# Hosted experts of the second joint stage in pairs of groups: eight products, one GELU, two groups' weights, eight accumulations

## The chip, the cores and the metric

The kernel runs on one core of a Trainium2 chip. A core has five engines that run side by side, each with its own in-order list of instructions: TensorE (PE, matrix products into PSUM), VectorE (DVE, elementwise work and reductions), ScalarE (ACT, activation functions and copies), GpSimd (POOL, here the issuer of gathers) and SyncE (SP, here the issuer of all other transfers). They wait for one another by semaphores only. Transfers run on 16 DMA engines that all issuers share. The metric is device time in microseconds, median over runs of the whole program; all data is float32.

## The reference

One layer of a hybrid encoder for 1024 prompt tokens and 8 x 16 sample tokens, nine tiles of 128 tokens in all. Each token passes a gated mLSTM branch (4 heads of 256) and a forgetting attention branch "FoX" (16 heads of 64), then an expert layer (PEER) and a gate. What matters here is the expert layer: each token picks 8 x 16 = 128 of 16384 single-neuron experts, each with a row `u` and a row `v` of 1024 numbers.

```python
idx = (take_along_axis(i1, j // PEER_TOPK) * PEER_KEYS + take_along_axis(i2, j % PEER_TOPK))
g = jax.nn.softmax(sc, axis=-1)
act = jax.nn.gelu(jnp.einsum('thkd,td->thk', u_tab[idx], xb).astype(jnp.float32), approximate=False)
return jnp.einsum('thk,thkd->td', (g * act).astype(xb.dtype), v_tab[idx])
```

and of the attention, for a block of 128 queries: `s = q k / 8 + c_q - c_k`, masked, `softmax(s)`, times `v`.

## The kernel before

The program is a sequence of stages. Six of the nine tiles have their experts gathered row by row by the class `Experts`: three in a first instance, `ex0`, "hosted" inside two joint stages, whose main work is something else, and three in the last joint stage (`stage_experts`), beside a dense form of the experts of the other three tiles. The first joint stage projects the input (`stage_project`) and hosts groups 0 to 51 of `ex0`. The second is the later part of attention (`stage_attend` with `b0` = 2, `b1` = 8: six query blocks, 96 steps) and hosts the remaining groups 52 to 95, 44 of them. It runs from about 1830 to 2525 us.

A group is four experts (`G` = 4) for 128 tokens, one token on each partition. For each expert POOL issues one indirect gather (`fetch`, L2558) that puts the rows `u` and `v`, 8 KB for each token and 1.05 MB together, into one of eight slots of `ex_uv`: two groups of four slots, group g in slots g % 2 * 4 and after. The fetch of group g + 2 into a slot waits until the accumulation of group g with that slot is counted in `added`. Then, on DVE, a group is nine units (`dve_unit`):

- units 0 to 3: one product each (L2599), the dot of `u` with the token's vector, into `ex_dot`; each waits for its slot's fetch (`uv_in`) and adds to `dotted`;
- unit 4: the weights (L2606), the four GELU values times the gates, after `geluted`;
- units 5 to 8: one accumulation each (L2615) of weight times `v` into `ex_acc`; each adds to `added`.

The GELU of a group is one ACT instruction on four numbers a partition (L2642), placed in ACT's list where unit 3 stands. Gelu and Exp are in different function tables, and an ACT_TABLE_LOAD stands before each change of table: one before a GELU, one before the next Exp, which is the softmax numerator (`act_exp`, L617).

Where hosted units stand among the attention's work is fixed as the program is written out. Each of the 96 steps has two halves; `hosted(s, half)` asks `units` for the half's share of the 44 x 9 = 396 units, 2 or 3 of them, in order of group and unit. In a step, DVE takes the maximum of the scores (L586) that PE left in PSUM, then the reciprocal of a sum, then a slot of the mLSTM, then the first half's units, another mLSTM slot and the second half's units. ACT's list has the Exp, the copies of the transposed probabilities (L625), the mLSTM's parts and, by the same `hosted`, the GELUs. Its list, too, is in order: what stands behind a GELU waits with it. SP loads the operands of later heads and chunks from `scratch_z` in pieces of 384 to 512 KB and stores results; POOL only issues fetches in this stage.

Of the kernel before, what the change touches and what calls it, by code (L numbers as in the profile page):

```python
# [18 lines left out]
ACT = mybir.ActivationFunctionType  # L19
# [608 lines left out]
class MlstmPrompt:  # L628
# [48 lines left out]
    def rows(self, c):  # L677
        t = self.c0 + 1 + c
        return slice(t * P, (t + 1) * P)

    def sp_load(self, sp, c):
        z, rows = self.z, self.rows(c)
        if c >= 1:
            self.wait_full(sp, self.group(c - 1, "q1"))
        sp.dma_start(self.q[:], z[rows, C_QM:C_KM]).then_inc(self.q_in, 16)
        if c >= 1:
            sp.wait_ge(self.kw_set, c * H_M)
        sp.dma_start(self.k[:], z[rows, C_KM:C_VM]).then_inc(self.k_in, 16)
        if c >= 1:
            sp.wait_ge(self.y_head, c * H_M)  # L690
        sp.dma_start(self.o[:], z[rows, C_OM:C_IM]).then_inc(self.o_in, 16)
        if c >= 1:
            self.wait_full(sp, self.group(c - 1, "c1", H_M - 1))
        sp.dma_start(self.v[:, :, 0:DM], z[rows, C_VM:C_OM].rearrange("t (h e) -> t h e", h=H_M)).then_inc(self.v_in, 16)
# [368 lines left out]
def stage_attend(nc, K, z, bias, cache_lf, gates, ck_last, C, m, T, b0, b1, ex=None, g0=0, g1=0):  # L1063

    with Stage(nc, f"att{b0}") as st:
        fx = FoxPrompt(nc, K, st, z, T, b0, b1)
        ml = MlstmPrompt(nc, K, st, z, gates, C, m, T, b0, b1)
        t0 = b0 + 1 if b0 else 0
        ga = Gates(K, st, z, bias, cache_lf, gates, ck_last, T, t0, b1 + 1 - t0, fx)
        STEPS = fx.STEPS  # L1070
        PER_STEP = ml.SLOTS * (b1 - b0) // STEPS
        assert PER_STEP == 2
        slot = lambda s, half: divmod(2 * s + half, ml.SLOTS)

        def hosted(s, half):
            return ex.units(g0, g1, 2 * s + half, 2 * STEPS) if ex and s < STEPS else []

        block = st.ctx.enter_context(nc.Block())

        @block.sync  # L1080
        def _(sp):
            ga.sp_load(sp)
            fx.sp_first(sp)
            ml.sp_load(sp, 0)
            if ex:
                ex.load_ahead(sp, g0)
            ga.sp_sums(sp)
            fx.sp_sums(sp)
            ga.sp_rest(sp)
            for s in range(STEPS):  # L1090
                fx.sp_step(sp, s)
                for half in range(2):
                    ml.sp_step(sp, *slot(s, half))
                    for g, unit in hosted(s, half):
                        ex.rows_unit(sp, g, unit)
            fx.sp_last(sp)
            ml.sp_last(sp)
            ga.sp_last(sp)
            if ex:
                ex.rows_end(sp, g1)  # L1100

        @block.tensor
        def _(pe):
            for g in range(len(fx.groups)):
                fx.pe_head(pe, 0, g)
            ga.pe_turn(pe)
            ga.pe_scores(pe)
            for s in range(STEPS + 1):
                if s < STEPS:
                    fx.pe_scores(pe, s)  # L1110
                    for hd, g in fx.heads_at(s):
                        fx.pe_head(pe, hd, g)
                    ml.pe_slot(pe, *slot(s, 0))
                if s >= 1:
                    for r in range(fx.rounds(s - 1)):
                        fx.pe_turn(pe, s - 1, r)
                if s < STEPS:
                    ml.pe_slot(pe, *slot(s, 1))
                if s >= 1:
                    for r in range(fx.rounds(s - 1)):  # L1120
                        fx.pe_mix(pe, s - 1, r)

        @block.scalar
        def _(act):
            for g in range(len(fx.groups)):
                fx.act_head(act, 0, g)
            ga.act_first(act)
            ga.act_probs(act)
            for s in range(STEPS + 2):
                if s >= 2:  # L1130
                    fx.act_y(act, s - 2)
                if s < STEPS:
                    for hd, g in fx.heads_at(s):
                        fx.act_head(act, hd, g)
                    ml.act_slot(act, *slot(s, 0))
                if 1 <= s <= STEPS:
                    for r in range(fx.rounds(s - 1)):
                        fx.act_probs(act, s - 1, r)
                if s < STEPS:
                    fx.act_exp(act, s)  # L1140
                for g, unit in hosted(s, 0):
                    ex.act_unit(act, g, unit)
                if s < STEPS:
                    ml.act_slot(act, *slot(s, 1))
                for g, unit in hosted(s, 1):
                    ex.act_unit(act, g, unit)

        @block.vector
        def _(dve):
            ga.dve_first(dve)  # L1150
            fx.dve_first(dve)
            ml.dve_first(dve)
            for s in range(STEPS + 1):
                if s < STEPS:
                    fx.dve_max(dve, s)
                if s >= 1:
                    fx.dve_invert(dve, s - 1)
                if s < STEPS:
                    ml.dve_slot(dve, *slot(s, 0))
                for g, unit in hosted(s, 0):  # L1160
                    ex.dve_unit(dve, g, unit)
                if s < STEPS:
                    ml.dve_slot(dve, *slot(s, 1))
                for g, unit in hosted(s, 1):
                    ex.dve_unit(dve, g, unit)
            if ex:
                ex.dve_close(dve, g1)
            ga.dve_last(dve)

        if ex:  # L1170
            @block.gpsimd
            def _(pool):
                ex.pool_span(pool, g0, g1)


class FoxSample:
# [3 lines left out]
    STEPS = 2 * NSEQ  # L1180
# [770 lines left out]
class Spread:  # L1951
# [25 lines left out]
    def units(self, i, a, b):  # L1977
        n = (i - self.FROM) * self.PER_STEP
        return range(n + a, n + b) if 0 <= n < self.UNITS else range(0)
# [544 lines left out]
class Experts:  # L2524

    G = 4
# [107 lines left out]
    def act_unit(self, act, g, unit):  # L2634
# [3 lines left out]
        if unit == self.G - 1:  # L2638
# [2 lines left out]
                act.wait_ge(self.weighed, g - 1)  # L2641
            act.activation(self.act[:, g % 2, :], self.dot[:, g % 2, :], ACT.Gelu).then_inc(self.geluted, 1)  # L2642

    def rows(self, t):
        return slice((self.tile0 + t) * P, (self.tile0 + t + 1) * P)

# [32 lines left out]
    def units(self, g0, g1, at, of):  # L2679
        n = (g1 - g0) * self.UNITS  # L2680
        for u in range(n * at // of, n * (at + 1) // of):
            yield g0 + u // self.UNITS, u % self.UNITS


class Dense:
# [500 lines left out]
```

## Time and profile before

| what | value |
|---|---|
| median of 3 runs | 4817.47 us (4817.3 to 4831.1) |
| profiled execution | 4826.2 us, span 4824.5 us |
| DVE busy, whole span | 2995.7 us (62%) |
| PE busy, whole span | 4326.6 us (90%) |
| ACT busy, whole span | 999.4 us (21%) |
| second joint stage | about 1830 to 2525 us |

The page of the profile gives busy times over the whole span and a chain of work that ended last; that chain reaches back only through the last stage. So a stage in the middle is read from its own stretch: busy time of each engine in it, the lists of waits ("A <- B" says that group A stood idle until group B released it), and the timeline of single instructions. An engine's idle time costs something only if the engine is the one that the stage waits for. Granted clock is the share of TensorE's full 2.4 GHz, 0.5 being its lower level of 1.2 GHz.

### The profile page before, as it was taken

Reading aid. Unit: us, or ns where it says so; the run is one execution under the profiler, and the core shown is the slowest. Engines: PE = TensorE matmul, PEld = TensorE weight load, DVE = VectorE, ACT = ScalarE, POOL = GpSimd, SP = SyncE. Lnnn points to the kernel's source line nnn. Section 1 sums busy time; section 2 is a strip of 40 time slices with the busy share of each in tenths; the row PEclk is TensorE's granted clock in tenths of the full one; section 3 lists DMA queues with packets and bytes.
Section 4 is the critical chain, followed back from the end, with each engine's and each line's share of the span. In section 5 each row is a group of like instructions: output and inputs, shape, how many; then the busy total and the mean of one; then the engine's idle time right before and its main releaser. Section 6 shows DMA issues by size and latency. Waiting matters only on the chain. (4 is left out here: it accounts for less than half of the span.)

```text
span 4824.5 us, 49007 instructions
## 1 busy us (share of the span) xinstructions
PE 4326.6 (90%) x16974; PEld 2667.5 (55%) x16974; DVE 2995.7 (62%) x6257; ACT 999.4 (21%) x1991; POOL 1260.4 (26%) x969
## 2 busy tenths in 40 slices
PE   8997686989999996888887988869999999999988
PEld 5555453665555554666664666654545454544534
DVE  1002241458777767888870587767888777777733
ACT  1113321111001104555551122220000000000023
POOL 0000031014444442333320000004444444444400
PEclk9998788999999997878878999989999999999999
DMA  4443496769999998988958777749999999999941
GB/s 169 143 147 98 146 320 265 284 236 421 385 382 391 384 355 284 335 307 313 343 209 331 278 267 262 241 155 418 419 407 408 419 419 419 416 414 409 418 177 58
DMA packets 363496, 1477.74 MB, mean 306 GB/s; under 512 B 38338, under 2 KB 178418, under 8 KB 242706
## 3 DMA queue, kind: packets, MB, share of 16 engines
q0 software_dynamic: 119872, 824.76, 42.4%
q1 hardware_dynamic: 193874, 625.13, 34.9%
q10 hardware_dynamic: 49536, 25.17, 1.7%
q8 instruction: 112, 1.84, 0.2%
q14 instruction: 102, 0.84, 0.0%
HBM read 1369.00 MB, written 115.38 MB: 308 GB/s over the span
## 5 line engine op out<-in xcount | busy, mean ns | idle before, releaser
L2558 POOL DMA_INDIRECT ex_uv<-in_uv,idx x768 | 1169.6, 1523 | 1683.4 <-DVE ex_acc L2615 1487.8
L2599 DVE CUSTOM_DVE_ANT_0 ex_uv<-ex_uv,ex_xp 128x1024 f32<-128x1024 f32 x768 | 912.9, 1221 | 296.2 <-DMA ex_uv<-in_uv,idx 249.6
L2615 DVE SCALAR_TENSOR_TENSOR ex_acc<-ex_uv,ex_wt,ex_acc 128x1024 f32<-128x1024 f32 x768 | 943.0, 1281 | 10.3 <-DVE C L897 3.2
L392 PE MATMUL proj_psum_acc<-proj_w,aT_later 128*128 128x385 f32 x2304 | 748.7, 487 | 8.0 <-DMA proj_w<-in_w_in 8.0
L2813 PE MATMUL exp_psum_dn<-exp_dn_big,exp_dn_gg 128*128 128x512 f32 x1536 | 686.6, 597 | 28.3 <-DVE exp_dn_gg L2769 28.1
L2804 PE MATMUL exp_psum_dn<-exp_dn_xT,exp_dn_big 128*128 128x384 f32 x2048 | 684.3, 488 | 7.6 <-DMA exp_dn_big<-in_ud 7.6
L392 PEld LDWEIGHTS proj_psum_acc<-proj_w,aT_later 128*128 128x128 f32 x2304 | 437.0, 190 | 319.3 <-DMA proj_w<-in_w_in 8.2
L2804 PEld LDWEIGHTS exp_psum_dn<-exp_dn_xT,exp_dn_big 128*128 128x128 f32 x2048 | 390.5, 191 | 307.7 <-issue 71.2
L2813 PEld LDWEIGHTS exp_psum_dn<-exp_dn_big,exp_dn_gg 128*128 128x128 f32 x1536 | 291.8, 191 | 379.1 <-issue 351.5
L301 PE MATMUL proj_psum_acc<-proj_w,aT 128*128 128x385 f32 x1152 | 377.1, 488 | 4.2 <-DMA proj_w<-in_w_in 2.3
L301 PEld LDWEIGHTS proj_psum_acc<-proj_w,aT 128*128 128x128 f32 x1152 | 218.3, 190 | 158.9 <-issue 4.5
L2242 PE MATMUL rt_psum_b<-rt_w,rt_yT 128*128 128x512 f32 x576 | 265.7, 623 | 31.8 <-ACT rt_yT L2335 24.3
L2277 PE MATMUL rt_psum_b<-rt_xT,rt_w 128*128 128x128 f32 x2304 | 265.8, 279 | 4.1 <-ACT rt_xT L2335 4.1
L2277 PEld LDWEIGHTS rt_psum_b<-rt_xT,rt_w 128*128 128x128 f32 x2304 | 264.7, 196 | 5.4 <-issue 5.4
L552 PE MATMUL att_psum_fs<-att_fkT,att_fqT 65*128 65x512 f32 (+3 forms) x384 | 197.0, 631 | 67.7 <-ACT att_fprob L617 48.7
L1240 POOL DMA_DIRECT2D scratch_ycat<-smp_sy x128 | 61.3, 487 | 678.1 <-DVE smp_sy L1340 678.1
L2782 ACT ACTIVATE exp_dn_gg<-exp_psum_dn 128x384 f32<-128x384 f32 x128 | 62.6, 489 | 838.9 <-PE exp_psum_dn L2804 838.2
L574 PE MATMUL att_psum_fy<-att_fv,att_fprobT 128*128 128x64 f32 x1152 | 174.8, 303 | 63.7 <-ACT att_fprobT L625 62.9
L2203 POOL DMA_DIRECT2D scratch_h<-rt_h x9 | 4.9, 541 | 800.2 <-DVE rt_h L2445 800.2
L2242 PEld LDWEIGHTS rt_psum_b<-rt_w,rt_yT 128*128 128x128 f32 x576 | 114.9, 202 | 175.1 <-issue 150.0
L574 PEld LDWEIGHTS att_psum_fy<-att_fv,att_fprobT 128*128 128x128 f32 x1152 | 157.5, 214 | 93.7 <-ACT att_fprobT L625 92.8
L402 ACT COPY proj_zs<-proj_psum_acc 128x385 f32<-128x385 f32 x144 | 68.9, 480 | 612.5 <-PE proj_psum_acc L392 612.5
(460 smaller groups left out, 4237.1 us busy)
## 6 DMA issues: line engine op xcount, KB each, us to landing
proj_w<-in_w_in SPq DMA_DIRECT2D x48, 1540.0 KB, 7.7
rt_w<-in_w_q SPq DMA_DIRECT2D x36, 2048.0 KB, 8.7
exp_dn_big<-in_ud SPq DMA_DIRECT2D x128, 512.0 KB
exp_dn_big<-in_vd SPq DMA_DIRECT2D x128, 512.0 KB, 8.0
scratch_z<-proj_zs SPq DMA_DIRECT2D x216, 192.5 KB, 2.0
rt_w<-in_w_br_m SPq DMA_DIRECT2D x18, 2048.0 KB, 9.4
rt_w<-in_w_br_f SPq DMA_DIRECT2D x18, 2048.0 KB, 10.6
rt_w<-in_w_out SPq DMA_DIRECT2D x18, 2048.0 KB, 8.2
```

Source lines behind the costliest of these rows:

```text
L301: mm = pe.matmul(acc[j % SLOTS][:, 0:CW], aT[:, k, t * P:(t + 1) * P], w[:, u % U, k, :], start=(k == 0), stop=(k == KD - 1))
L392: mm = pe.matmul(acc[j % SLOTS][:, 0:CW], aT[:, k, t * P:(t + 1) * P], w[:, u % U, k, :], start=(k == 0), stop=(k == KD - 1))
L402: act.copy(zs[:, j % SLOTS, :], acc[j % SLOTS][:, 0:CW]).then_inc(read, 1)
L552: pe.matmul(out[:, c:c + w], self.qT[:, hd % 2, b * P:(b + 1) * P], self.kT[:, hd % 2, c:c + w], start=True, stop=(c + w != n))
L574: mm = pe.matmul(self.y_ps[:, 0:DF], self.probT[:, c * P:(c + 1) * P], self.v[:, i % 2, c, e * DF:(e + 1) * DF], start=(c == 0), stop=(c = ...
L2242: mm = pe.matmul(b[:], yT[:, u * KD + k, :], ws[:, k, :], start=(k == 0), stop=(k == KD - 1))
L2277: mm = pe.matmul(b[:, c * P:(c + 1) * P], ws[:, k, c * P:(c + 1) * P], xT[:, k, :], start=(k == 0), stop=(k == KD - 1))
L2558: pool.indirect_dma_start(self.uv[:, slot, :], None, self.uv_tab, bass.IndirectOffsetOnAxis(ap=self.idx[:, at:at + 1], axis=0)).then_inc(s ...
L2599: dve.tensor_tensor_reduce(self.uv[:, slot, 0:D], self.uv[:, slot, 0:D], self.xp[:], 1.0, 0.0, ALU.mult, ALU.add, self.dot[:, g % 2, j:j + ...
L2615: dve.scalar_tensor_tensor(out=self.acc[:, j % 2, :], in0=self.uv[:, slot, D:2 * D], scalar=self.wt[:, g % 2, j:j + 1], in1=self.acc[:, j ...
L2804: mm = pe.matmul(self.banks[3][:, at:at + self.TOKENS], self.big[:, q % 4, k * P:(k + 1) * P], self.xT[:, k, :], start=(k == 0), stop=(k = ...
L2813: mm = pe.matmul(self.banks[t][:, n * 512:(n + 1) * 512], self.gg[:, 4 + q % 4, t * P:(t + 1) * P], self.big[:, 4 + q % 4, n * 512:(n + 1) ...
```

## The change

In the second joint stage the units come from a new generator `paired`, which orders the 18 units of two groups as 8 products, 2 weights, 8 accumulations. ACT runs `act_pair` there: one GELU for both groups on eight numbers a partition, placed where the eighth product stands, adding 2 to `geluted`. DVE's and SP's calls take the new order from `hosted` without other edits. The first joint stage and the last one keep `units` and `act_unit`. `fetch`, the eight slots and POOL's list are as before.

```diff
         def hosted(s, half):
-            return ex.units(g0, g1, 2 * s + half, 2 * STEPS) if ex and s < STEPS else []
+            return ex.paired(g0, g1, 2 * s + half, 2 * STEPS) if ex and s < STEPS else []
...
                 for g, unit in hosted(s, 0):
-                    ex.act_unit(act, g, unit)
+                    ex.act_pair(act, g, unit)
...
+    def act_pair(self, act, g, unit):
+
+        t, r = divmod(g, self.PER_TILE)
+        if unit == 0 and r == 0:
+            self.act_tile(act, t)
+        if unit == self.G - 1 and g % 2 == 1:
+            act.wait_ge(self.dotted, (g + 1) * self.G)
+            if g >= 3:
+                act.wait_ge(self.weighed, g - 1)
+            act.activation(self.act[:], self.dot[:], ACT.Gelu).then_inc(self.geluted, 2)
...
+    def paired(self, g0, g1, at, of):
+
+        G, two = self.G, 2 * self.UNITS
+        n = (g1 - g0) * self.UNITS
+        for u in range(n * at // of, n * (at + 1) // of):
+            pair, k = divmod(u, two)
+            if k < 2 * G:
+                e, unit = divmod(k, G)
+            elif k < 2 * G + 2:
+                e, unit = k - 2 * G, G
+            else:
+                e, unit = divmod(k - 2 * G - 2, G)
+                unit += G + 1
+            yield g0 + 2 * pair + e, unit
```

On DVE before, about a fifth into the stage, accumulations of a group are followed by products of the next one, whose rows have been in the other four slots for a while (`ex_uv` 4 to 7):

```order
L2615 SCALAR_TENSOR_TENSOR ex_acc<-ex_uv,ex_wt,ex_acc 128x1024 [waits ex0_added] x3
L586 TENSOR_REDUCE att_fnmax<-att_psum_fs 128x1 [waits proj0_gain_in,proj0_cut]
L593 RECIPROCAL att_finv<-att_ftotal 128x1 [waits proj0_rooted,proj0_gain_in]
L2599 ISA ex_uv,ex_dot<-ex_uv,ex_xp 128x1024 [waits ex0_geluted,ex0_uv_in4]
L2599 ISA ex_dot 128x1
L2599 ISA ex_uv,ex_dot<-ex_uv,ex_xp 128x1024 [waits ex0_uv_in5]
```

On DVE now, near the same place, from the eighth product of a pair (slot 7) to the first of the next pair:

```order
L2599 ISA ex_uv,ex_dot<-ex_uv,ex_xp 128x1024 [waits ex0_uv_in7]
L2599 ISA ex_dot 128x1
L2606 TENSOR_TENSOR ex_wt<-ex_act,gate 128x4 [waits ex0_added,ex0_geluted]
L897 SCALAR_TENSOR_TENSOR C<-C,att_mw,att_psum_m 128x257 [waits proj0_summed]
L897 SCALAR_TENSOR_TENSOR C<-C,att_mw,att_psum_m 128x257 [waits proj0_read]
L2606 TENSOR_TENSOR ex_wt<-ex_act,gate 128x4 [waits att0_m_c_set,ex0_added,ex0_geluted]
L2615 SCALAR_TENSOR_TENSOR ex_acc<-ex_uv,ex_wt,ex_acc 128x1024 [waits ex0_added,ex0_weighed]
L586 TENSOR_REDUCE att_fnmax<-att_psum_fs 128x1 [waits proj0_gain_in,proj0_cut]
L593 RECIPROCAL att_finv<-att_ftotal 128x1 [waits proj0_rooted,proj0_gain_in]
L2615 SCALAR_TENSOR_TENSOR ex_acc<-ex_uv,ex_wt,ex_acc 128x1024 [waits ex0_added] x3
```

The first accumulation of a pair, which frees the first slot, has moved behind all eight products. (The names of other stages' semaphores in these rows, such as `proj0_cut`, are numbers used again; they stand for this stage's `scored` and others.)

On ACT before, around one GELU, with a table load for it and one for the next Exp. The load waits for `weighed` only, and the GELU for `dotted`:

```order
L617 ACTIVATE att_fprob,att_ftotal<-att_psum_fs,att_fnmax 128x512 [waits proj0_squared,proj0_ident_cut,proj0_reduced]
L2642 ACT_TABLE_LOAD [waits ex0_weighed]
L2642 ACTIVATE ex_act<-ex_dot 128x4 [waits ex0_dotted]
L602 ACTIVATE att_fy<-att_psum_fy,att_finv 128x64 [waits proj0_meaned,proj0_squared]
L610 ACTIVATE att_fkT<-att_psum_ft 64x512 [waits proj0_cut,proj0_ident_cut]
L625 COPY att_fprobT<-att_psum_ft 128x512 [waits proj0_meaned,proj0_ident_cut]
L617 ACT_TABLE_LOAD [waits proj0_squared,proj0_ident_cut]
L617 ACTIVATE att_fprob,att_ftotal<-att_psum_fs,att_fnmax 128x640 [waits proj0_reduced]
```

On ACT now, around one GELU of a pair:

```order
L617 ACTIVATE att_fprob,att_ftotal<-att_psum_fs,att_fnmax 128x384 [waits proj0_squared,proj0_ident_cut,proj0_reduced]
L2653 ACT_TABLE_LOAD [waits ex0_weighed,ex0_dotted]
L2653 ACTIVATE ex_act<-ex_dot 128x8
L602 ACTIVATE att_fy<-att_psum_fy,att_finv 128x64 [waits proj0_meaned,proj0_squared]
L610 ACTIVATE att_fqT<-att_psum_ft 64x256 [waits proj0_cut,proj0_ident_cut]
```

Both waits now stand on the table load, in all 22 places. ACT has 66 instructions fewer in all, 1659 rows in the order against 1725.

## Rows read from the trace of the kernel before

**Rows 1.** The stage's stretch: busy us by engine (instructions), clock, DMA share, GB/s

```profile
1830.00:2525.00 695.00, 583.58 (x2887) 447.03 (x2887) 599.71 (x1056) 392.08 (x746) 236.07 (x168) 0.81 0.82 304
```

**Rows 2.** Lines of DVE in the stage: busy us, mean ns, idle us

```profile
L2615 DVE SCALAR_TENSOR_TENSOR ex_acc<-ex_uv,ex_wt,ex_acc 128x1024 f32<-128x1024 f32 x176 | 218.8, 1280 | 4.6 <-DVE C L897 3.2
L2599 DVE CUSTOM_DVE_ANT_0 ex_uv<-ex_uv,ex_xp 128x1024 f32<-128x1024 f32 x176 | 208.6, 1218 | 3.9 <-DVE C L897 3.0 <-DVE ex_acc L2575 0.7
```

**Rows 3.** Waits in the stage: waiting group, releaser: us in total, times, longest

```profile
DVE ex_wt L2606 <- ACT ex_act L2642: 36.2, 30, 3.3
DVE att_fnmax L586 <- PE att_psum_fs L554: 36.0, 31, 3.5
```

**Rows 4.** Lines of ACT in the stage

```profile
L2642 ACT ACT_TABLE_LOAD x44 | 56.5, 1283 | 1.1 <-ACT att_mwD L925 0.3
L617 ACT ACT_TABLE_LOAD x43 | 55.2, 1283 | 0.8
...
L2642 ACT ACTIVATE ex_act<-ex_dot 128x4 f32<-128x4 f32 x44 | 9.0, 205 | 27.0 <-DVE ex_dot L2599 26.7
```

**Rows 5.** Timeline, ACT and DVE around two GELUs: start us, us, engine, line

```profile
2116.62 0.21 ACT L2642 ACTIVATE ex_act<-ex_dot 128x4 f32<-128x4 f32 x1
...
2116.86 0.16 DVE L2606 TENSOR_TENSOR ex_wt<-ex_act,gate 128x4 f32<-128x4 f32 x1 [3.34 <-ACT ex_act L2642]
...
2145.92 1.22 DVE L2599 CUSTOM_DVE_ANT_0 ex_uv<-ex_uv,ex_xp 128x1024 f32<-128x1024 f32 x1
...
2147.18 0.20 ACT L2642 ACTIVATE ex_act<-ex_dot 128x4 f32<-128x4 f32 x1 [0.29 <-DVE ex_dot L2599]
...
2148.45 1.28 DVE L2615 SCALAR_TENSOR_TENSOR ex_acc<-ex_uv,ex_wt,ex_acc 128x1024 f32<-128x1024 f32 x1
```

**Rows 6.** Timeline of POOL, fetches at which bursts begin or end

```profile
1852.81 1.74 POOL L2558 DMA_INDIRECT ex_uv<-in_uv,idx  x1 [50.34 <-DVE ex_acc L2615]
...
2135.70 1.74 POOL L2558 DMA_INDIRECT ex_uv<-in_uv,idx  x1 [9.52 <-DVE ex_acc L2615]
...
2150.01 0.94 POOL L2558 DMA_INDIRECT ex_uv<-in_uv,idx  x1 [7.54 <-DVE ex_acc L2615]
...
2164.92 1.74 POOL L2558 DMA_INDIRECT ex_uv<-in_uv,idx  x1 [7.42 <-DVE ex_acc L2615]
...
2169.44 0.94 POOL L2558 DMA_INDIRECT ex_uv<-in_uv,idx  x1 [0.30 <-issue]
...
2487.97 0.94 POOL L2558 DMA_INDIRECT ex_uv<-in_uv,idx  x1 [7.54 <-DVE ex_acc L2615]
```

**Rows 7.** Stretches around two bursts of fetches; last columns: DMA share, GB/s

```profile
2138.00:2139.00 1.00, 0.17 (x2) 0.03 (x1) 1.00 (x2) 0.99 (x2) 0.68 (x1) 1.00 0.87 164
2139.00:2148.00 9.00, 8.38 (x44) 6.74 (x44) 8.76 (x20) 4.40 (x12) 2.87 (x2) 0.81 1.00 411
2149.00:2150.00 1.00, 0.56 (x5) 0.25 (x2) 1.00 (x2) 0.56 (x2) 0.00 (x0) 1.00 0.06 25
2151.00:2180.00 29.00, 24.10 (x98) 17.77 (x98) 25.21 (x42) 14.65 (x28) 9.16 (x8) 0.72 0.98 377
```

**Rows 8.** DMA queues in the stage: packets, MB, share of 16 engines

```profile
q0 software_dynamic: 24192, 176.17, 66.0%
q1 hardware_dynamic: 32459, 34.42, 15.4%
```

**Rows 9.** The tile ex_uv in the stage: who waited for it, and landings

```profile
  POOL ex_uv L2558: 430.1, 82
...
DMA to landing us min/median/max: 6.2/8.3/14.2
```

**Rows 10.** Timeline of SP's queue, first and last of five issues

```profile
2154.25 0.34 SPq L698 DMA_DIRECT2D scratch_ycat<-att_my  x1
...
2156.93 0.53 SPq L694 DMA_DIRECT2D att_mv<-scratch_z  x1
```

**Rows 11.** Waits of DVE from 3500 to 4600 us, the last joint stage

```profile
DVE ex_uv L2599 <- DMA ex_uv<-in_uv,idx: 201.1, 116, 3.8
```

More of the change, by code:

```diff
@@ L1145, in _ @@
                 for g, unit in hosted(s, 1):
-                    ex.act_unit(act, g, unit)
+                    ex.act_pair(act, g, unit)
         @block.vector
```

## The prediction

> **What bounds the kernel now.** I read four views in this order. First the stretches: the second joint stage is the one from about 1830 to 2525 us, and in it DVE is busy 599.7 of 695 us, PE 583.6 at a granted clock of 0.81, ACT 392.1, and the DMA engines 0.82 of the time at 304 GB/s [rows 1]. So DVE has the least idle time, with the DMA engines not far behind. The DVE lines show why: 176 products of 1.22 us and 176 accumulations of 1.28 us fill most of it, and neither waited more than 5 us in all for anything [rows 2]. Then the waits: what DVE does wait for is the GELU (36.2 us in 30 waits) and the scores of PE (36.0 us in 31) [rows 3]. POOL's 430.1 us for the accumulations [rows 9] are no loss by themselves: POOL issues the fetches, and a fetch may start only when its slot was accumulated. That wait decides when transfers begin. Last the transfers: DVE never waits for a fetch in this stage; the list of who waited for `ex_uv` has only POOL in it [rows 9].
>
> The stage is thus set by DVE in order, with a period that the fetch bursts show: first bursts of the groups at 1852.81 and 2487.97, which is group 54 to group 95 [rows 6]. 635.2 us over 41 groups are 15.5 us for a group, 31.0 us for a pair.
>
> **What is removed.** 44 GELUs become 22. Each has a table load of 1.283 us and forces one back for the next Exp: 44 and 43 loads, 111.7 us of ACT [rows 4]. 22 GELUs and 44 loads go, about 4.5 + 56.5 = 61 us of ACT. ACT is busy 56% of the stage, so these 61 us are worth only what somebody waits for them: of DVE's 36.2 us behind the GELU, and of its 36.0 us behind PE, whose scores wait for the Exp. One thing takes part of the first back. Before, the table load stands ahead of the wait for the dots (its row in the order has only `weighed`), so it runs while the last product does; in the changed order all 22 loads carry the wait for `dotted` too. So each GELU now answers 1.28 (load) + 0.04 (the product's end, 2145.92 + 1.22, to ACT at 2147.18) + 0.24 (GELU's start to the weights' start, 2116.62 to 2116.86) = 1.6 us after the last product, never earlier [rows 5]. 22 times 1.6 is 35 us; where attention work stands between the last product and the weights it covers about a third, so some 25 us of wait stay of 36. With at most 10 us of the PE waits, the gain on this side is 10 to 20 us, 0 at worst.
>
> **What is moved.** The number of products, accumulations and fetches stays, and so do buffers, semaphores and POOL's queue. But the slots come free in one burst of eight, and are needed in one burst of eight.
> Today the last of four fetches of a group lands 1.28 (first accumulation) + 0.28 (its end at 2149.73 to POOL at 2150.01) + 2.3 (POOL at 2135.70 to the first bytes, engines 0.87 full from 2138 on) + 10.7 (four fetches, until the engines fall to 0.06 at 2149) + about 0.8 = 15.4 us after the group's first accumulation [rows 5 to 7]. The 0.8 is last byte to semaphore: the fastest landing, 6.2 us, less 2.3 and one transfer of 2.6, bounds it at 1.3 [rows 9], and I take the middle of 0.2 to 1.3. The fetch is due 16 of a pair's 18 units later, 16/18 x 31.0 = 27.5 us. Twelve us of reserve explain why nobody waits.
> After the change the eighth fetch lands 1.28 + 0.28 + 2.3 + 21.0 + 0.8 = 25.7 us after the first accumulation. The 21.0 lies between 20.4 (8.39 MB at the steady 411 GB/s) and 21.4 (twice 10.7) [rows 7]. It is due when seven accumulations and seven products more have run, 15/18 x 31.0 = 25.8 us. The reserve is gone, before any other transfer is counted.
>
> The ring that this closes is: first accumulation, slot, fetches, eighth product, GELU, weights, first accumulation. Its length without other traffic: 25.7 + 1.22 (product) + 1.6 (load and GELU) + 0.35 (two weights) + 0.7 (attention work that stands before the first accumulation; 0 to 2) = 29.5 us. There are 21 such rings between 22 pairs: 620 us.
> Other traffic is the term that tips it. SP's queue takes 15.4% of 695 us, 107 us of all engines [rows 8]. The two 3 MB copies out at the stage's start, some 19 us at the same 3.1 us per MB (107 us for 34.4 MB), mostly come before the first ring: 88 us stay. That this traffic does lengthen a burst is seen once in the trace: five issues of 512 KB from 2154.25 to 2156.93 [rows 10] fall among the eight fetches issued 2150.01 to 2169.44 [rows 6], and the engines are full for 29 us, 2151 to 2180 [rows 7]: 21 and 8. That stretch is what the changed kernel's whole cycle would be. The engines move fetches for 21 of 29.5 us of a ring, so 0.71 of the 88, 62 us, falls into bursts (40 to 88 as ends) and adds its full length.
> Sum: 620 + 62 = 682 us against 21 x 31.0 = 651 today, +31. And a ring is as long as the longer of DVE's need and the transfers': today's pairs run from 29.2 (2135.70 to 2164.92) [rows 6] upward, and long pairs don't always meet the traffic. I add 10 us for that (0 to 20). **+41 us**, with the GELU gain already in it, since the ring contains the new GELU.
> Ends: with 20.4, 0.2 and no attention work the ring is 27.6 us, 580 + 40 = 620, under DVE's own 651, so that end is rival B. With 21.4, 1.3 and 2.0 it is 31.7, 666 + 88 = 754, +103.
>
> The trace shows round-robin in effect only by such a stretch. The Trainium skill says it outright ("DMA: Bandwidth & Descriptors", section SWDGE vs HWDGE vs iDMA): inside each DMA engine the queues fed by GpSimd and by SP are served in turn, so SP's packets slow the fetches; by that rule the 62 us are right. The same page (Anatomy of one DMA) puts a fixed 2.0 us on a transfer where I have 2.3 + 0.8 = 3.1 from rows; by its figure, an estimate, the sum would be 21 x 1.1 = 23 us lower, +18.
>
> What a late fetch looks like is in this kernel already: in the last joint stage, with the same ring of eight slots but dense traffic beside it, DVE waits 201.1 us for fetches, 116 times [rows 11].
>
> **Rivals.**
> A, the forecast: the fetches set the ring. +41 us.
> B, the fetches still come in time, and the GELU side counts. For it: reserve and need are equal within 0.1 us, the average DMA share is only 0.82, and bursts leave gaps to other traffic. Against it: the 29 us stretch. It gives 10 to 20 us less, 4802, and can't give much more, since all of DVE's waits for ACT and PE are 72 us and the loads now stand behind the dots. It decides if traffic in bursts is under about 30 us and the ring under 29. The Trainium skill speaks for this one ("ScalarE: Activation LUTs", Table sets: the hidden batching unit): batch activation calls by table set. It prices a switch at 2.66 us with the drain; the trace has 1.283 for the load alone [rows 4] and no drain that it shows. By the page's figure, as an estimate, 44 loads would be 117 us of ACT, still mostly beside DVE's work.
> C, both effects nearly cancel: 4803 to 4832.
> D, stalls spread: while DVE waits at the eighth product ACT waits for `dotted` with it, and behind it in ACT's order stand the copies and the Exp of the next step, so PE runs dry and its clock, 0.81 on average now, falls further. A further 2.5 us in each ring are +50, 4910.
> That the change does not do what it says is excluded by the order: ACT has 66 rows less, 22 GELUs and 44 loads.
>
> **Numbers.** The profiled run's span is 4824.5 us, its time 4826.2, 9 above the median of 4817.5; I add differences to the median. A: 4817.5 + 41 = 4859, rounded up to 4860. Chances: A 0.64, B 0.12, C 0.18, D 0.06. Below 4803 lies most of B, some 0.1; above 4905 D and the end of A, 0.08. The range is 4803 to 4905. Faster by over 0.3% (14 us, what a measurement of this kernel can tell from none) 0.12, within 0.18, slower 0.70.
>
> **What would show it.** In the changed trace: waits of DVE's products for the fetch, some 40 to 100 us where there are none, most at the fourth to eighth slot; POOL's gaps before a burst about 15 us instead of 7 to 10; DMA share no higher than 0.8 with longer full stretches; 22 table loads at the GELU and about as many fewer at the Exp; DVE's wait for the GELU 20 to 35 us; a pair every 32 to 33 us. The prediction is wrong if products don't wait (then B), if eight fetches queued together move faster than 411 GB/s or slower, or if the stage is longer by PE's waits and not by the fetches (D).

## The result, and the profile after

| | median us | spread | ratio to before |
|---|---|---|---|
| before | 4817.5 | 4817.3 to 4831.1 | |
| changed | 4863.7 | 4861.3 to 4869.2 | 1.0086 (1.0069 to 1.0103) |

The changed kernel is 46 us slower by these medians and 41 by the ratio of 1.0086; against the medians of before in the later rounds, 4823.8 to 4826.0, it is 38 to 40. Forecast were 4860 us, 4803 to 4905, and 0.70 for slower. The profiled execution has a span of 4862.0 us, 37.5 more than that of before, whose profiled execution was 9 us above its median.

The stretch of the second joint stage comes first, with the same columns as [rows 1]. It now ends about 2571 us.

```profile
1830.00:2571.00 741.00, 589.18 (x2885) 454.62 (x2883) 599.55 (x1055) 331.08 (x677) 226.96 (x168) 0.79 0.75 284
```

DVE is busy for the same 600 us as in [rows 1], in 741 us instead of 695. ACT has lost 61 us of work (392.1 to 331.1), as worked out ahead, and the stage is still longer by 46 us (the profiled execution of before lost most of its 9 us outside the stage): ACT's work was not what it waited for. The DMA engines are busy 0.75 of the time and not 0.82, so bandwidth over the stage did not run out either. What changed is who waits (group that waits <- releaser: us in total, times, longest):

```profile
POOL ex_uv L2558 <- DVE ex_acc L2615: 474.1, 61, 58.6
...
ACT L2653 <- issue: 62.5, 19, 9.2
...
DVE ex_uv L2599 <- DMA ex_uv<-in_uv,idx: 45.6, 42, 3.0
...
DVE att_fnmax L586 <- PE att_psum_fs L554: 40.4, 26, 3.6
...
ACT att_fprob L617 <- DVE att_fnmax L586: 38.2, 20, 6.3
...
DVE ex_wt L2606 <- ACT ex_act L2653: 31.4, 22, 2.6
```

The third line is the loss. No product waited for a fetch before [rows 9]; now they wait 45.6 us, in 42 places. The waits for the GELU fell only from 36.2 to 31.4 us, and those for the scores rose from 36.0 to 40.4 [rows 3]. 45.6 - 4.8 + 4.4 = 45.2 us, which is the stage's 46. The table load's 62.5 us (L2653, put down to "issue") is the load standing behind the wait for the dots, as its row in the order said: 22 loads at the GELU, and L617's down from the 43 of [rows 4] to 25.

```profile
L617 ACT ACT_TABLE_LOAD x25 | 32.1, 1283 | 0.4
...
L2653 ACT ACT_TABLE_LOAD x22 | 28.2, 1283 | 62.7 <-issue 62.5
```

One ring in full, from the timeline (start us, duration, engine, line), shows how the two bursts meet:

```profile
2288.24 1.28 DVE L2615 SCALAR_TENSOR_TENSOR ex_acc<-ex_uv,ex_wt,ex_acc 128x1024 f32<-128x1024 f32 x1
...
2289.79 0.94 POOL L2558 DMA_INDIRECT ex_uv<-in_uv,idx  x1 [17.55 <-DVE ex_acc L2615]
...
2301.06 1.27 DVE L2615 SCALAR_TENSOR_TENSOR ex_acc<-ex_uv,ex_wt,ex_acc 128x1024 f32<-128x1024 f32 x1
...
2302.25 1.22 DVE L2599 CUSTOM_DVE_ANT_0 ex_uv<-ex_uv,ex_xp 128x1024 f32<-128x1024 f32 x1
...
2302.60 1.68 POOL L2558 DMA_INDIRECT ex_uv<-in_uv,idx  x1 [0.59 <-issue]
...
2308.25 1.22 DVE L2599 CUSTOM_DVE_ANT_0 ex_uv<-ex_uv,ex_xp 128x1024 f32<-128x1024 f32 x1 [0.55 <-DMA ex_uv<-in_uv,idx]
...
2310.90 1.23 DVE L2599 CUSTOM_DVE_ANT_0 ex_uv<-ex_uv,ex_xp 128x1024 f32<-128x1024 f32 x1 [1.42 <-DMA ex_uv<-in_uv,idx]
...
2313.58 1.22 DVE L2599 CUSTOM_DVE_ANT_0 ex_uv<-ex_uv,ex_xp 128x1024 f32<-128x1024 f32 x1 [1.44 <-DMA ex_uv<-in_uv,idx]
...
2316.25 1.23 DVE L2599 CUSTOM_DVE_ANT_0 ex_uv<-ex_uv,ex_xp 128x1024 f32<-128x1024 f32 x1 [0.50 <-DMA ex_uv<-in_uv,idx]
...
2317.55 1.28 ACT L2653 ACT_TABLE_LOAD   x1 [0.84 <-issue]
...
2318.84 0.21 ACT L2653 ACTIVATE ex_act<-ex_dot 128x8 f32<-128x8 f32 x1
...
2319.09 0.24 DVE L2606 TENSOR_TENSOR ex_wt<-ex_act,gate 128x4 f32<-128x4 f32 x2 [1.60 <-ACT ex_act L2653]
...
2319.28 2.48 DVE L2615 SCALAR_TENSOR_TENSOR ex_acc<-ex_uv,ex_wt,ex_acc 128x1024 f32<-128x1024 f32 x2
```

The first accumulation starts at 2288.24 and POOL fetches into its slot at 2289.79, 1.55 us later: the 1.28 + 0.28 of the sum. The eighth accumulation starts at 2301.06, the eighth fetch is issued at 2302.60, and the first product of the next pair at 2302.25, before that fetch is even issued. Products 1 to 4 find their rows there. The fifth, sixth, seventh and eighth each wait, 0.55, 1.42, 1.44 and 0.50 us: DVE consumes a row every 1.2 us and the DMA engines bring one every 2.7. The last product starts 28.0 us after the first accumulation, then load, GELU and weights answer 1.60 us after it, exactly the figure of the forecast, and the next first accumulation is at 2319.28: a ring of 31.0 us. The same pair took 27.9 us in the kernel before (2256.60 to 2284.54). The sum has the eighth product at 25.7 us without other traffic; SP's queue took 8.5% of the 26 us from 2290 to 2316, 2.2 us, and 25.7 + 2.2 = 27.9 is what the ring shows:

```profile
q0 software_dynamic: 1152, 8.39, 84.3%
q1 hardware_dynamic: 1320, 0.67, 8.5%
```

Over the stage the first bursts of POOL give the mean:

```profile
1857.06 1.73 POOL L2558 DMA_INDIRECT ex_uv<-in_uv,idx  x1 [58.63 <-DVE ex_acc L2615]
...
2519.39 0.93 POOL L2558 DMA_INDIRECT ex_uv<-in_uv,idx  x1 [18.23 <-DVE ex_acc L2615]
```

2519.39 less 1857.06 is 662.3 us, and for 20 rings 33.1 us a pair, against 31.0 before [rows 6] and 32.5 in the sum. POOL's gap before a burst grew from the 7 to 10 us of [rows 6] to 15 and more, here 18.2. And with eight fetches queued together a fetch lands later than in [rows 9], with the same bytes and issues:

```profile
DMA to landing us min/median/max: 8.8/11.3/15.3
```

### The profile page after: what moved, and what is told of

The parts are those of the page before. It is cut to its first block and busy times, and to the rows that moved or that the text cites. A ratio compares the mean times of both kernels' runs of the same rounds, so it can differ in the third digit from the quotient of the medians.

```text
span 4862.0 us, 48919 instructions
## 1 busy us (share of the span) xinstructions
PE 4324.0 (89%) x16974; PEld 2669.7 (55%) x16974; DVE 2995.5 (62%) x6257; ACT 940.9 (19%) x1925; POOL 1245.6 (26%) x969
## 5 line engine op out<-in xcount | busy, mean ns | idle before, releaser
L2558 POOL DMA_INDIRECT ex_uv<-in_uv,idx x768 | 1154.8, 1504 | 1741.4 <-DVE ex_acc L2615 1538.8
L2839 PE MATMUL exp_psum_dn<-exp_dn_big,exp_dn_gg 128*128 128x512 f32 x1536 | 684.9, 596 | 30.1 <-DVE exp_dn_gg L2795 30.0
L2830 PEld LDWEIGHTS exp_psum_dn<-exp_dn_xT,exp_dn_big 128*128 128x128 f32 x2048 | 390.0, 190 | 306.4 <-issue 69.5
L2242 PE MATMUL rt_psum_b<-rt_w,rt_yT 128*128 128x512 f32 x576 | 266.7, 625 | 32.2 <-ACT rt_yT L2335 24.3
L574 PE MATMUL att_psum_fy<-att_fv,att_fprobT 128*128 128x64 f32 x1152 | 178.2, 307 | 87.3 <-ACT att_fprobT L625 86.4
L574 PEld LDWEIGHTS att_psum_fy<-att_fv,att_fprobT 128*128 128x128 f32 x1152 | 161.2, 218 | 117.5 <-ACT att_fprobT L625 116.4
```

The costliest lines, as they stand in the source:

```text
L574: mm = pe.matmul(self.y_ps[:, 0:DF], self.probT[:, c * P:(c + 1) * P], self.v[:, i % 2, c, e * DF:(e + 1) * DF], start=(c == 0), stop=(c = ...
L2242: mm = pe.matmul(b[:], yT[:, u * KD + k, :], ws[:, k, :], start=(k == 0), stop=(k == KD - 1))
L2558: pool.indirect_dma_start(self.uv[:, slot, :], None, self.uv_tab, bass.IndirectOffsetOnAxis(ap=self.idx[:, at:at + 1], axis=0)).then_inc(s ...
L2830: mm = pe.matmul(self.banks[3][:, at:at + self.TOKENS], self.big[:, q % 4, k * P:(k + 1) * P], self.xT[:, k, :], start=(k == 0), stop=(k = ...
L2839: mm = pe.matmul(self.banks[t][:, n * 512:(n + 1) * 512], self.gg[:, 4 + q % 4, t * P:(t + 1) * P], self.big[:, 4 + q % 4, n * 512:(n + 1) ...
```

## The experiments

Three rounds each, five for the last; each against runs of the kernel before on the same chip, whose medians were 4823.8 to 4826.0 us (4817.5 for the first line). So lines are best compared by their ratios. The waits are DVE's in the second joint stage, from each run's own trace.

| run | median us | ratio (95%) | fetch | GELU | scores |
|---|---|---|---|---|---|
| changed | 4863.7 | 1.0086 (1.0069 to 1.0103) | 45.6 | 31.4 | 40.4 |
| order_only | 4858.0 | 1.0066 (1.0050 to 1.0083) | 39.3 | 10.1 | 48.1 |
| load_early | 4844.4 | 1.0044 (1.0027 to 1.0061) | 47.9 | 12.5 | 36.2 |
| exp_after | 4839.5 | 1.0033 (1.0021 to 1.0044) | 55.2 | 8.6 | 30.0 |
| exp_before | 4784.8 | 0.9921 (0.9898 to 0.9945) | none | 11.7 | 24.9 |
| half_before | 4824.7 | 0.9995 (0.9984 to 1.0006) | none | 37.0 | 37.4 |
| half_after | 4826.3 | 1.0005 (0.9994 to 1.0017) | 3.4 | 36.9 | 43.6 |
| traffic_before | 4827.3 | 1.0002 (0.9991 to 1.0014) | none | 36.7 | 34.7 |
| traffic_after | 4879.3 | 1.0113 (1.0096 to 1.0131) | 55.7 | 31.6 | 39.5 |
| split_after | 4827.5 | 1.0005 (0.9995 to 1.0014) | none | 29.0 | 39.9 |
| split_early | 4818.5 | 0.9988 (0.9977 to 0.9999) | none | 16.4 | 43.9 |
| skew_before | 4825.6 | 1.0001 (0.9991 to 1.0010) | 32.2 | 1.1 | 39.3 |
| skew_split | 4819.3 | 0.9988 (0.9978 to 0.9998) | none | 0.2 | 65.8 |

### The order alone, with two GELUs a pair

```diff
-                    ex.act_pair(act, g, unit)
+                    ex.act_unit(act, g, unit)
```

(in the changed kernel, both halves)

> The new order of the units alone, with one GELU for each group as before (two for a pair). Theory A (the eight slots come free in one burst and the eight fetches set a ring of about 33 us a pair): the ring is as in the changed kernel, so the time is about the same, 4855 to 4870 us, and DVE's products wait 35 to 55 us for fetches. The table loads are back (44 at the GELU) and cost at most 10 us more than in the changed kernel. Rival (the single late GELU blocks ACT's list for 62 us and starves PE): with a GELU for each group ACT is as before and the time returns to 4815 to 4830.

Measured: 4858.0 us. The waits:

```profile
DVE att_fnmax L586 <- PE att_psum_fs L554: 48.1, 35, 3.5
...
ACT ex_act L2642 <- DVE ex_dot L2599: 41.0, 24, 4.4
...
DVE ex_uv L2599 <- DMA ex_uv<-in_uv,idx: 39.3, 40, 3.0
...
DVE ex_wt L2606 <- ACT ex_act L2642: 10.1, 10, 2.7
```

The order of the units alone makes the loss; what the merged GELU adds, 1.0086 against 1.0066, can't be told from nothing, since the intervals overlap. I had expected the opposite sign, up to 10 us more with 44 loads. Two GELUs leave DVE 10.1 us of waits behind them instead of 31.4, since the first of a pair is long done and the second has its load ahead of the wait for the dots again: it is the GELU, not the load, that waits for them (`ex_act` L2642, 41.0 us). The rival, ACT's list blocked by one late GELU, would have brought 4815 to 4830 and falls.

### Half the bytes

```diff
-            pool.indirect_dma_start(self.uv[:, slot, :], None, self.uv_tab, bass.IndirectOffsetOnAxis(
+            few = self.tile0 == 0 and g >= EARLY + 2
+            dst = self.uv[:, slot, 0:D] if few else self.uv[:, slot, :]
+            tab = self.T["tab_u"] if few else self.uv_tab
+            pool.indirect_dma_start(dst, None, tab, bass.IndirectOffsetOnAxis(
```

(`tab_u` is a table of the u rows alone, laid out beside the joined one; in both kernels)

> The kernel before, where the fetches of the second joint stage's groups from 54 on bring only the u half of a row, 4 KB instead of 8 (the accumulations then read older v rows). DVE's work is unchanged. Nobody waited for a fetch, so the time is that of before within 5 us; DMA share falls to about 0.5. It is the partner for the next run.

> The changed kernel, with the same half fetches. Theory A: eight fetches take about 11 us instead of 21, they land 10 us before they are due, products wait for none, and the time is set by DVE again: below the kernel before by the GELU side, 4800 to 4815. Rival (late GELU, ACT and PE): the loss stays, 4850 or more.

Measured: 4824.7 and 4826.3 us; waits in the changed order, with half the bytes:

```profile
DVE att_fnmax L586 <- PE att_psum_fs L554: 43.6, 25, 3.7
...
DVE ex_wt L2609 <- ACT ex_act L2656: 36.9, 22, 4.1
...
ACT att_fprob L617 <- DVE att_fnmax L586: 20.3, 20, 2.2
...
DVE ex_uv L2602 <- DMA ex_uv<-in_tab_u,idx: 3.4, 4, 1.4
```

With the bytes halved, and nothing of DVE's, ACT's or PE's lists changed, the loss is gone: 1.0005 instead of 1.0086. So it lies in the transfers. But I had 4800 to 4815 here, because the GELU side should then have paid 10 to 20 us. It paid nothing. Its waits are 36.9 us in 22 places where half the bytes in the old order have 37.0; the 22 loads behind the dots come to 35 us of that by the forecast's 1.6. The scores cost 43.6 instead of 37.4, in a profiled execution that was 9.5 us above its median (4835.9), so these waits are at their upper end.

### More traffic beside it

```diff
             for s in range(STEPS):
+                if ex and s % 8 == 4:
+                    c = s // 8 * P
+                    sp.dma_start(T["spare"][c:c + P, :], ex.uv_tab[c:c + P, :]).then_inc(spare, 16)
                 fx.sp_step(sp, s)
```

> The kernel before with twelve more copies of 1 MB from DRAM to DRAM on SP's queue, spread over the second joint stage, 31 to 38 us of all DMA engines at the 2.6 to 3.1 us per MB of the trace. The old order has 12 us of reserve for each fetch: no more than 8 us above before.

> The changed kernel with the same twelve copies. Theory A: 0.71 of their 31 to 38 us falls into bursts and adds its full length, 22 to 27 us above the changed kernel, 4886 to 4891. Rival (transfers don't set the ring): as little as in the kernel before, under 8 us.

Measured: 4827.3 us, no more than before, and 4879.3 us, above the changed kernel by 0.0027 in the ratio, 13 us, or 15.6 us in the medians. Each ratio has an interval of 8 us to both sides, so the difference is 13 us give or take some 12. What the copies took is read in the kernel before, without and with them, from 1830 to 2575 us, where all other transfers are the same (SP's queue: packets, MB, share of 16 engines):

```profile
q1 hardware_dynamic: 36832, 49.14, 19.3%
```

```profile
q1 hardware_dynamic: 36526, 61.84, 23.2%
...
scratch_spare<-in_uv SPq DMA_DIRECT2D x12, 13.3
```

The direction is as theory A has it: the old order hides the copies, the new one does not. The size was less than 22 to 27 us. One reason is in these rows: the copies took 23.2 - 19.3 = 3.9% of 745 us, 29 us for 12.7 MB, that is 2.3 us for a MB and not 2.6 to 3.1. The other would be the share that falls into bursts: 13 to 16 of 29 us is about 0.5, where I had 0.71, but with 12 us of uncertainty this run alone does not exclude 0.71.

### What the table loads are worth

```diff
-            act.activation(self.act[:], self.dot[:], ACT.Gelu).then_inc(self.geluted, 2)
+            act.activation(self.act[:], self.dot[:], ACT.Exp).then_inc(self.geluted, 2)
```

(in the changed kernel; in the one before, the same for its GELU of one group)

> The kernel before with Exp in the place of the GELU in the second joint stage (the experts' values of that stage are other ones). It shows what all 87 table loads cost before, the most that batching GELUs could ever bring. By DVE's 36 us of waits for the GELU and 36 us for PE I expect 25 to 40 us less than before, 4778 to 4793. If the loads were covered by DVE's work, as the rival to any gain has it, under 10 us less.

> The changed kernel with Exp in the place of the GELU in the second joint stage, so that no function table is changed for the experts there (the experts' values of that stage are thus other ones). Theory A: the ring loses its table load (1.28 us, 21 times) and ACT another load per pair beside it: 4830 to 4842. Products still wait for fetches, 40 to 60 us. Rival (late GELU blocks ACT and PE): the same or smaller, since the wait for the dots stays where it is: 4855 or more.

Measured: 4784.8 and 4839.5 us, both as expected. In the kernel before, without any switch of tables for the experts:

```profile
DVE att_fnmax L586 <- PE att_psum_fs L554: 24.9, 19, 3.5
...
DVE ex_wt L2606 <- ACT ex_act L2642: 11.7, 26, 1.5
```

39 us are what 86 loads cost the kernel before (its trace has 101 in the stage, that of exp_before 15): DVE's wait for the GELU is shorter by 24.5 us and that for the scores by 11.1. The loads are thus a real cost, and the change removed half of them. In the changed kernel the remaining 42 (57 against 15) cost 24 us by the medians (26 by the ratios). Both orders without switches differ by 55 us, more than the 40 to 46 with them: the transfers' loss is the larger the faster the rest is.

### The load ahead of the wait

```diff
+            act.activation(self.warm[:], self.gate[:, 0:1], ACT.Gelu)
             act.wait_ge(self.dotted, (g + 1) * self.G)
```

> The changed kernel, with a GELU on one number a partition just ahead of the wait for the dots, so that the table load runs before the eighth product has ended. Theory A: each of some 21 rings is shorter by the load, 1.28 us, less the extra instruction's 0.2: 20 to 25 us less than the changed kernel, 4839 to 4845. Rival (transfers are late by other traffic, and what follows the product is covered by attention work): no more than 8 us less.

Measured: 4844.4 us, 19 less than the changed kernel. The GELU waits fell from 31.4 to 12.5 us:

```profile
DVE ex_uv L2600 <- DMA ex_uv<-in_uv,idx: 47.9, 48, 2.8
...
DVE att_fnmax L586 <- PE att_psum_fs L554: 36.2, 27, 3.6
...
DVE ex_wt L2607 <- ACT ex_act L2655: 12.5, 15, 2.7
```

A 1.28 us load behind the wait, 22 times, was a term of the ring at most of its length (28 us, less 22 times 0.2 for the extra instruction, against 19). This fits a ring that goes through the GELU and not only through the transfers: products still wait 47.9 us, and the whole ring became shorter.

### Slots that come free in halves

```diff
+            pool.wait_ge((self.dotted, self.added)[part], (g - 2) * G + j + 1)
+            cols = slice(part * D, (part + 1) * D)
+            pool.indirect_dma_start(self.uv[:, slot, cols], None, self.T[("tab_u", "tab_v")[part]], ...
...
+            if self.tile0 == 0 and g >= EARLY + 2:
+                dve.wait_ge(self.v_in[slot], ((g - EARLY) // 2) * 16)
```

(in the changed kernel; the second piece ahead of each accumulation)

> The changed kernel, with each fetch of the second joint stage (groups from 54 on) in two, from a table of u and one of v: the u half of a slot is fetched again as soon as its product is done, the v half as soon as its accumulation is. Same bytes, same slots, twice the issues on POOL (336 instead of 168). Theory A (slots come free too late and all at once): u rows have a whole cycle's half more time, DVE's waits for fetches fall from 45 us to under 10, and the time falls to that of the half fetches, 4820 to 4832. Rival (bandwidth as such, or POOL's issue time of 16 x 1.3 to 2.0 us a pair, sets it then): 4850 or more.

> The last kernel with the early table load beside it. Theory A says that both terms are real and add: 20 us less than the split alone, 4800 to 4812, the first form of the pairing that is faster than before. If the load is covered once the fetches are in time: as the split alone.

Measured: 4827.5 and 4818.5 us. In the first no product waits for a fetch, with all bytes:

```profile
POOL ex_uv L2569 <- DVE ex_acc L2634: 110.9, 58, 5.2
POOL ex_uv L2569 <- issue: 79.4, 257, 0.8
...
DVE att_fnmax L586 <- PE att_psum_fs L554: 39.9, 26, 4.7
...
DVE ex_wt L2623 <- ACT ex_act L2672: 29.0, 17, 2.8
```

All bytes and the same eight slots, but u rows are asked for half a cycle sooner, and the loss is gone. So it was the moment at which a slot came free and not bandwidth. POOL issued 336 fetches instead of 168 and still waited 110.9 us for DVE, so the rival of the issue time falls. The early load on top gave 8 to 9 us, not 20, and the result, 0.9988, is only just under before: DVE's wait for the GELU fell by 12.6 us while that for the scores rose by 4.0.

### The old order, skewed by two products

```diff
+            order += [(g, unit) for unit in range(0 if first else early, self.G)]
+            order += [] if last else [(g + 1, unit) for unit in range(early)]
+            order += [(g, unit) for unit in range(self.G, self.UNITS)]
```

(in the kernel before, `early` = 2, instead of the order of `units`)

> The kernel before, one GELU a group, but with the first two products of the next group between a group's last product and its weights (not across a tile's end). DVE then has 2.4 us of work while ACT loads the table and does the GELU; slots still come free four at a time. Theory A (what a GELU costs is DVE's wait behind it, and fetches have 12 us of reserve): DVE's 36 us of waits for the GELU fall to under 12, PE's 36 us stay, 15 to 28 us less than before. Rival (the wait only moves to the scores): under 5 us less.

Measured: 4825.6 us, no gain. The waits:

```profile
DVE att_fnmax L586 <- PE att_psum_fs L554: 39.3, 30, 3.6
...
DVE ex_uv L2599 <- DMA ex_uv<-in_uv,idx: 32.2, 19, 3.9
...
DVE ex_wt L2606 <- ACT ex_act L2642: 1.1, 2, 0.9
```

The 36 us behind the GELU are gone, as meant, but 32.2 us of waits for fetches stand in their place. I had overlooked that a product moved ahead of four accumulations is due six units after its slot's fetch could start and not thirteen; all 19 waits are at such products. It is the fault of the change under study once more, in small: order gives to one wait what it takes from another. The last run puts the split fetches under this order.

> The skewed order of one GELU a group together with the split fetches. In the skewed order alone DVE's wait for the GELU was gone (36 to 1 us), but its products waited 32 us for fetches, since a product moved ahead of four accumulations has less reserve. Theory A (order decides how late a slot's fetch may be, split fetches give the reserve back): waits for fetches under 8 us, for the GELU under 5, and the gain that the skewed order missed appears: 20 to 35 us less than before, 4790 to 4805. Rival (DVE's waits move on to PE's scores whatever is removed): DVE's wait for the scores grows from 36 to 60 us or more and the time stays within 8 us of before.

Measured: 4819.3 us, 0.9988. Neither fetch nor GELU is waited for now, 0.2 us in all:

```profile
ACT att_fprobT L625 <- PE att_psum_ft L560: 108.9, 63, 7.8
...
DVE att_fnmax L586 <- PE att_psum_fs L554: 65.8, 43, 3.8
...
PE att_psum_fs L552 <- ACT att_fprob L617: 44.2, 40, 2.2
...
ACT att_fprob L617 <- DVE att_fnmax L586: 3.6, 4, 2.0
```

This expectation failed, and the rival named in it holds: DVE's wait for the scores rose from 36.0 to 65.8 us, and of 36 us removed some 6 came out at the end. So DVE's waits behind the GELU, which the forecast counted as time to be gained, were not what set the pace of the kernel before. By its dependencies there is a second ring under the first: with scores of up to 1024 columns there is only one score buffer (`SBUFS` is 1), so `pe_scores` waits for the Exp of the step before, the maximum waits for the scores and the Exp for the maximum. Whatever DVE gains beside this ring it would spend waiting for it. But the trace shows only a part of it at work. DVE waits for the scores, and PE's scores wait for the Exp (44.2 us); the Exp waits for DVE's maximum only 3.6 us in all, so ACT comes to it after the maximum is there. What ACT waits for most is PE's transposes, ahead of its copies of the probabilities, 108.9 us. That the pace is set between ACT and PE is thus argued and not shown. That the table loads count in it is shown by exp_before, where both waits of DVE fell and the whole 39 us came out. A second score buffer was not tried.

Two runs, split_early and skew_split, are about 0.1% below the kernel before, with intervals that end at 0.9999 and 0.9998. That is at the edge of what can be told, and far below what the 39 us of exp_before leave to gain.

## Why the prediction held

The likeliest case was the right one, by its mechanism and within 4 us in size.

- **The fetches set the ring.** Confirmed from both sides: half the bytes take the loss away (half_after), and so do the same bytes asked for sooner (split_after). Waits for fetches were put at 40 to 100 us and are 45.6, at the fifth to eighth product in the ring above, as said; over the stage 35 of the 42 waits are at the sixth to eighth.
- **The ring's length.** 32.5 us with its traffic, or 33.0 with the 10 us for long pairs; 33.1 measured. Of the terms, 1.28 + 0.28 and the 1.6 us of load and GELU are met to 0.05 us. In the ring shown, no attention work stands between weights and accumulation, where I had put 0.7. The 21 rings, each from a pair's first accumulation to the next pair's in DVE's timeline, are not alike. Products wait for a fetch in 15 of them. Mean length in us:

| rings | before | changed | half_after | split_after |
|---|---|---|---|---|
| all 21 | 31.0 | 33.1 | 31.3 | 31.1 |
| the 15 with waits for fetches in the changed kernel | 30.4 | 32.5 | 30.1 | 30.2 |
| the 6 without | 32.4 | 34.4 | 34.1 | 33.5 |

In the 15, what the new order adds goes away with the late fetches, some 35 us in all. In the 6 most of it stays: they are long by waits for scores and for the GELU, as DVE's waits show in one of 35.9 us, from 2352.07 to 2387.98:

```profile
DVE att_fnmax L586 <- PE att_psum_fs L554: 4.6, 3, 2.4
DVE ex_wt L2606 <- ACT ex_act L2653: 1.6, 1, 1.6
```

With fetches in time, the short rings make up for the long ones; with late fetches they can't.
- **Other traffic.** 62 us, from 0.71 of 88, was too much. In the changed kernel's trace SP's queue took some 45 us in the 21 stretches from a burst's first bytes (3.9 us after the first accumulation) to the start of the eighth product, 0.52 of the 88. So another term was too small. It is the 10 us for rings that are longer than the transfers make them: 21 rings took 694 us, and 620 + 45 leaves 29, above the 0 to 20 that it was given. Its source was a wrong reading: the pairs of the kernel before don't run from 29.2 us upward but from 25.5 to 35.7. The total is right partly because these two errors cancel, which is luck.
- **The GELU side.** "The gain on this side is 10 to 20 us, 0 at worst": it is the worst case. ACT's 61 us went as counted, and DVE's wait for the GELU came out at 31.4 us, in the range of 20 to 35. But the up to 10 us of PE's waits came with the wrong sign (36.0 to 40.4). The step that failed is the assumption that ACT's time and DVE's wait behind PE fall together. The single late GELU is not the reason: order_only, without it, has 48.1 us. What the rows show is that DVE's maximum comes later: the Exp waits for it 10.5 us before, 25.1 in order_only, 38.2 in the changed kernel and, with half the bytes, 20.3 in the new order against 10.6 in the old. And skew_split shows that DVE's waits for the GELU could fall by 36 us with a gain of only 5 or 6.
- **The rivals.** B failed in both halves: fetches are late, and with them in time there is nothing to gain (half_after 1.0005, where it gave 4802 us). D's chain is in the trace, but not its price: the Exp's wait for the maximum grew from 10.5 to 38.2 us and PE's for ACT's copies (L574) from 46.2 to 69.5, while DVE's for the scores cost 4 us more, not 50. The clock fell only from 0.81 to 0.79. The rule of the Trainium skill to batch activation calls by table set ("ScalarE: Activation LUTs", Table sets: the hidden batching unit) is right that the switches cost time here, 39 us for 86 loads by exp_before, or 0.45 us for each of 1.283. It does not say that the batch may cost more than its loads: the order that it took made a reserve of twelve us into none.

The rule that queues are served in turn inside a DMA engine ("DMA: Bandwidth & Descriptors", SWDGE vs HWDGE vs iDMA, in the Trainium skill) agrees with traffic_after's direction, as any sharing of the engines would; no run tells how the queues share them. The fixed 2.0 us that the same page puts on a transfer (Anatomy of one DMA) would have given +18 as an estimate, and the measured +41 to +46 is nearer to the sum from rows.

## What to carry to other kernels

Batching work that reads a ring of buffers also batches the moments at which buffers come free. Write down for each transfer when its slot is free and when its data is due, in the old order and in the new; where the reserve shrinks to nothing, other transfers beside the burst make its data late, whatever the average bandwidth says. And when DVE waits at two places in turn, taking one away may only lengthen the other: look for what both depend on before counting the first as a gain.

## What the runs showed of the hardware

A copy from DRAM to DRAM took 2.3 us of all engines for a MB (traffic_before), less than the 2.6 of the row gathers from DRAM to SBUF (66.0% of 695 us for 176.17 MB [rows 8]) and less than the 3.1 of SP's other transfers. POOL issued a gather of 128 rows of 4 KB in 1.41 us on average in half_before, as the 8 KB rows in the kernel before (1.41): in these runs the issue time goes by rows, not by bytes. And the same fetch lands after 8.3 us in bursts of four and after 11.3 in bursts of eight.
